# Causal convolution of the mLSTM queries and keys: read from its PSUM bank instead of from a padded copy in SBUF

## The reference, cut to what matters

```python
def causal_conv(x, w, b):
    K = w.shape[0]                                    # 4 taps
    S = x.shape[1]                                    # 256 tokens
    xp = jnp.pad(x, ((0, 0), (K - 1, 0), (0, 0)))
    return sum(xp[:, j:j + S] * w[j] for j in range(K)) + b
...
qk = jax.nn.silu(causal_conv(ml_qk, conv_w[l], conv_b[l]))   # ml_qk: 1024 channels
m_q, m_k = jnp.split(qk, 2, axis=-1)
```

## Time and profile before

| | |
|---|---|
| device time, median of 3 runs | 500.75 us (499.75 to 503.14) |
| the profiled execution | 500.96 us |
| its span, first to last instruction | 499.2 us |
| mean granted TensorE clock | 0.951 |
| busy: PE, DVE, ACT, POOL | 427.1, 165.3, 173.9, 157.9 us |
| DMA | 163.30 MB, mean 327 GB/s |

### The profile page before, as it was taken

One profiled execution on the slowest core, in us unless ns is written; L12 is line 12 of the kernel. 1 busy time (PEld: TensorE's weight loads), 2 busy tenths in 40 slices (PEclk: granted clock), 3 DMA queues, 4 the chain that ended last, 5 costly groups with the idle time before them and its releaser, 6 DMA issues.

```text
span 499.2 us, 8883 instructions
## 1 busy us (share of the span) xinstructions
PE 427.1 (86%) x3772; PEld 318.2 (64%) x3772; DVE 165.3 (33%) x345; ACT 173.9 (35%) x305; POOL 157.9 (32%) x126
## 2 busy tenths in 40 slices
PE   1837999899999999999996989898989788594983
PEld 0415989789899999997984745463636254261541
DVE  0224302899984232178236111111111111102014
ACT  1216451744549358534335331212122112030122
POOL 0008996574946865997700000000000000000000
PEclk9978999998999999999997999998989889799799
DMA  7999969579589347557999699999999999999942
GB/s 290 389 358 394 304 184 387 184 269 330 170 281 318 120 168 251 171 169 266 421 420 421 253 391 425 420 421 421 423 420 420 421 420 422 421 420 422 418 196 85
DMA packets 55725, 163.30 MB, mean 327 GB/s; under 512 B 7058, under 2 KB 33924, under 8 KB 43268
## 3 DMA queue, kind: packets, MB, share of 16 engines
q1 hardware_dynamic: 50528, 159.53, 82.7%
q10 hardware_dynamic: 5156, 3.17, 2.2%
HBM read 161.64 MB, written 1.05 MB: 326 GB/s over the span
## 4 chain that ended last, share of the span: by engine, by line
PE 70%; DMA 15%; DVE 5%; SPq 4%; issue 2%; ACT 2%; POOL 1%; DVEq 0%
PE bank L1271 33%; DMA ring<-in_w_e 11%; PE bank L1585 10%; PE bank L1597 7%; PE bank L1553 6%; PE bank L1542 5%; DMA ring<-in_w_ada 4%; PE bank L1224 3%; SPq L376 2%; SPq L365 1%; POOL ring_r L413 1%; DVE gm L1017 1%; PE bank L1508 1%; PE bank L1631 1%; PE bank L1560 1%
## 5 line engine op out<-in xcount | busy, mean ns | idle before, releaser
L413 POOL TENSOR_TENSOR ring_r<-ring,ring_r 128x512 fp32r<-128x512 f32 x120 | 157.6, 1348 | 89.1 <-ACT ring_r L448 88.9
L1271 PE MATMUL bank<-ring_r 128*128 128x256 f32 x832 | 111.3, 285 | 4.7 <-DVE att L837 2.3
L1271 PEld LDWEIGHTS bank<-ring_r 128*128 128x128 f32 x832 | 103.8, 191 | 7.4 <-issue 4.3
L670 ACT ACTIVATE raw<-bank,sm 128x128 f32<-128x128 f32 x72 | 27.2, 458 | 157.6 <-PE bank L1553 157.6
L448 ACT ACTIVATE ring_r<-ring 128x2048 fp32r<-128x2048 f32 x30 | 57.4, 1912 | 44.0 <-PE bank L1271 26.2
L1585 PE MATMUL bank<-ring,raw 128*32 128x256 f32 x640 | 57.0, 410 | 6.1 <-DMA hT<-in_w_e 6.1
L1149 DVE TENSOR_TENSOR tmp<-bank,tmp 128x256 f32<-128x256 f32 x8 | 3.4, 425 | 123.1 <-ACT tmp L678 123.1
L1585 PEld LDWEIGHTS bank<-ring,raw 128*32 128x32 f32 x640 | 28.2, 117 | 22.4 <-issue 10.7
L1553 PEld LDWEIGHTS bank<-const,xn 128*128 128x128 f32 x288 | 35.8, 199 | 9.0 <-issue 7.1
L1597 PE MATMUL bank<-ring,WT 128*32 128x512 f32 x160 | 37.5, 654 | 2.6 <-DVE WT L1154 2.6
L1224 PE MATMUL bank<-ring,sm 128*32 128x256 f32 x384 | 27.3, 433 | 13.9 <-DMA ring<-in_w_ada 13.7
(11 more groups left out here) (309 smaller groups left out, 591.7 us busy)
## 6 DMA issues: line engine op xcount, KB each, us to landing
ring<-in_w_e SPq DMA_DIRECT2D x60, 1024.0 KB, 24.7
ring<-in_w_ada SPq DMA_DIRECT2D x24, 1024.0 KB, 11.0
ring<-in_w_in SPq DMA_DIRECT2D x22, 1024.0 KB, 8.8
extra<-in_w_e SPq DMA_DIRECT2D x11, 1024.0 KB, 18.6
late<-in_w_e SPq DMA_DIRECT2D x5, 1024.0 KB, 19.3
qkT<-in_w_e SPq DMA_DIRECT2D x5, 1024.0 KB, 20.4
mqk<-in_w_e SPq DMA_DIRECT2D x5, 1024.0 KB, 26.2
gm<-in_w_e SPq DMA_DIRECT2D x5, 1024.0 KB, 26.1
```

The costliest lines, as they stand in the source:

```text
L413: pool.tensor_tensor(ring_r[:, slot_of(n), sl], ring[:, slot_of(n), sl], hi(d)[:, sl].bitcast(F32), ALU.subtract).then_inc(s["w_lo"], 1)
L670: ins = act.activation(xg[:, b, k, :], token_bank[:, j * P:(j + 1) * P], ACT.Identity, bias=S("B2p", KD)[:, k:k + 1], scale=S("A2p", KD)[: ...
L1271: ins = pe.matmul(out, left(k), right(k), start=(i == 0 and k == 0), stop=(i == 2 and k == nk - 1))
```

## The change

The padded copy is gone. The convolution reads the bank: the last tap (weight 3, no shift) is written to all 256 columns, and each other tap j, shifted back by 3 - j columns, is added to columns 3 - j and on, so that no zeros are needed. DVE's last instruction of `conv(i)` now releases the bank of `ml{i}`, ACT's four copies (L510) and POOL's clearing of the pads (L406) are dropped, and `conv(2)` and `conv(3)` are moved from behind the decay arguments to the place right behind `combine(3)`. ACT's Silu waits for the bank's release instead of for a semaphore of its own.

```diff
         def _(pool):
-            pool.memset(raw[:, :, 0:3], 0.0).then_inc(s["pads"], 1)
...
-                act.wait_ge(s["pads"], 1)
-                act.wait_ge(*full(f"ml{h}"))
-                release(act.activation(raw[:, 2 * h:2 * h + 2, 3:T + 3],
-                                       pb(f"ml{h}")[:].rearrange("p (a n) -> p a n", a=2), ACT.Copy), f"ml{h}")
                 split(9 + h)
...
-                act.wait_ge(s["conv_out"], i + 1)
+                act.wait_ge(*free(f"ml{i}"))
...
             def conv(i):
 
-                dve.wait_ge(*free(f"ml{i}"))
-                for k in (2 * i, 2 * i + 1):
-                    link(dve.tensor_scalar(mqk[:, k, :], raw[:, k, 3:T + 3], col("conv_w", 24 + k), col("conv_b", k),
-                                           ALU.mult, ALU.add))
+                job = f"ml{i}"
+                dve.wait_ge(*full(job))
+                for a in range(2):
+                    k, seq = 2 * i + a, pb(job)[:, a * T:(a + 1) * T]
+                    link(dve.tensor_scalar(mqk[:, k, :], seq, col("conv_w", 24 + k), col("conv_b", k), ALU.mult, ALU.add))
                     for j in range(3):
-                        ins = dve.scalar_tensor_tensor(out=mqk[:, k, :], in0=raw[:, k, j:j + T],
-                                                       scalar=col("conv_w", 8 * j + k), in1=mqk[:, k, :],
+                        back = 3 - j
+                        ins = dve.scalar_tensor_tensor(out=mqk[:, k, back:T], in0=seq[:, 0:T - back],
+                                                       scalar=col("conv_w", 8 * j + k), in1=mqk[:, k, back:T],
                                                        op0=ALU.mult, op1=ALU.add)
                         if j < 2:
                             link(ins)
-                    if k % 2 == 0:
+                    if a == 0:
                         link(ins)
-                ins.then_inc(s["conv_out"], 1)
+                release(ins, job)
...
             conv(1)
             combine(3)
+            conv(2)
+            conv(3)
...
             rows(2)
-            conv(2)
-            conv(3)
```

More of the change, by code:

```diff
@@ L506, in _ @@
                                    accum_out=S(f"Z{h % 2}", 4)[:, 2 * c + 1:2 * c + 2]).then_inc(s["pexp"], 1)
-                act.wait_ge(s["pads"], 1)
-                act.wait_ge(*full(f"ml{h}"))
-                release(act.activation(raw[:, 2 * h:2 * h + 2, 3:T + 3],
-                                       pb(f"ml{h}")[:].rearrange("p (a n) -> p a n", a=2), ACT.Copy), f"ml{h}")
                 split(9 + h)
-            act.wait_ge(s["pads"], 2)
+            act.wait_ge(s["pads"], 1)
             for i in range(2):
```

## The result

| | before | after |
|---|---|---|
| device time, median of 6 runs each | 500.25 us (498.77 to 503.14) | 508.51 us (505.97 to 513.99) |
| ratio after to before | | 1.0147, 95% interval [1.0121, 1.0173] |
| the profiled execution | 500.96 us | 509.3 us |
| its span | 499.2 us | 507.4 us |
| mean granted TensorE clock | 0.951 | 0.931 |

The kernel is slower by 1.5%, some 7.4 us. The forecast was 11.9 us slower, 512.9 us.

A forecast was written before the change was run, and what follows sets the result against it. PE was taken to bound the stretch. A later mv1 (10.46 us) plus its low clock (1.67) less the ada(2) wait (0.25) gave 11.9 us on 500.96, thus 512.9 us; range 508.5 to 516.5, more than 8 in 10.

The forecast's parts named there:

- PE is the bound, and every new wait is paid in full: From 89.9 to 224 us PE waits only 0.3 us, so any new wait of PE reaches the end.
- DVE as releaser of the banks: PE waits for convolution ends: some 5 us before mv0, 3 to 4 us before mv1.
- The third stall: PE's wait before the second transpose, aT1, for conv(2) to end at 133.2 us; 1 to 2 us.
- What a convolution costs: On DVE, an undisturbed convolution from PSUM takes 4.26 us (3.6 to 4.6) against 3.91, unstretched by POOL.
- the second rival: POOL stretches the PSUM reads of conv(2) and conv(3), 4.3 us more: 517.2 us; chance 0.06.
- DVE's line: DVE's queue of combine, columns and convolutions, followed with times from the trace before, ends conv(3) at 137.4 us.
- The term of 10.46 us: mv1 waits for conv(3) and starts at 137.45 instead of 126.99 us; this last stall holds the sum.
- the fourth rival: Faster: conv(1) would have to end before 118.94 us, but adaT4 makes 120.8 the earliest; chance 0.02.
- The clock: After PE's idle, mv1 begins at 1.2 GHz and takes 1.67 us more.
- the prediction's own signs of being wrong: mv0 near 119, convolutions at 1 us an operation, first expert load near 230 despite full waits, or clock 1.00 at mv1.
- the full one: Rival: the clock stays at 2.4 GHz in mv1, 511.2 us, or 509.2 with cheaper convolutions; chance 0.25.
- The saving of 0.25 us at `ada(2)`: PE's wait at ada(2) for own_columns to L904 on DVE goes away, 0.25 us less.

The follow-up runs named there:

- e4: Kernel after with another DVE order: conv(0) to conv(2) first, conv(3) behind columns(A2, 4), then combine(2), combine(3) and own_columns; 501.08 us, ratio 1.001.
- e1: Kernel before with only conv(2) and conv(3) moved right behind combine(3), still reading ACT's padded copies; 515.29 us, ratio 1.0311.
- before_again: Kernel before, unchanged, one more execution for a second trace; 506.43 us, beside 23 others with a median of 501.04 us.
- after_again: Kernel after, unchanged, measured and traced a second time; 508.21 us, ratio 1.0178.
- e2: Kernel before with conv(0) and conv(1) reading the bank; ml2 and ml3 still copied, conv(2) and conv(3) at their old place; 505.28 us, ratio 1.0097.
- e3: Kernel after with 24 extra matmuls of 256 columns before aT0, result thrown away; 508.7 us, and 510.66 us when run again.
- e7: Kernel before, copies kept, with the grow chain behind scores(1) and cols with the decay arguments ahead of conv(1); 502.4 us, ratio 1.002.
- e5: e4 with the chain of small operations on grow moved behind scores(1); 502.41 us, ratio 1.0036.
- e8: e7 with PE's small jobs spread: cols behind ml1, Mb0 behind ada(4), Mb1 behind ml2; 501.11 us, ratio 1.0012.
- e9: e8 with the router bias, which releases the bank of rb, ahead of conv(2); 498.78 us, ratio 0.9969.

## Why the prediction was right and where it was wrong

**PE is the bound, and every new wait is paid in full: right.** Of the waits at `mv0` and `mv1`, and of the slower `mv1`, nothing was absorbed: 7.02 later at `mv1`, 1.72 for its clock, and 0.3 for the wait at `ada(2)` that went, give 8.4; the first expert load is 8.34 late, the span 8.2. All other kernels keep the same 267 to 270 us from that load to the end of the span.

**The mechanism, DVE as releaser of the banks: right.** PE waits at `mv0` and `mv1` on the convolution's last operation, as said (3.5 and 2.7 us, where some 5 and 3 to 4 were forecast), and e4, in which only DVE's order differs, takes the loss back. The third stall, 1 to 2 us before the second transpose, did not come: `conv(2)` had ended at 129.7, ahead of `aT0`.

**What a convolution costs: right.** Forecast 4.26 us, measured 4.23 from the start of `conv(1)` to its end (118.41 to 122.64). `tensor_scalar` 544 ns, 535 assumed; `scalar_tensor_tensor` 481 ns, 485 assumed. No stretching under POOL, so the second rival (517.2 us) falls; e1 shows such stretching with the operands in SBUF, 515.29 us. The fixed extra cost for PSUM that the Trainium skill gives (VectorE: DVE Perf Modes, "The TRN2 errata — SBUF-src ops pay a fixed extra latency per instruction") and the prediction weighed is not seen for `scalar_tensor_tensor` (481 ns from PSUM, 485 from SBUF); `tensor_scalar` takes 130 ns more from PSUM (544 against 414).

**DVE's line: this is the step that failed.** The prediction read the durations of DVE's queue off one trace and kept them for the changed kernel. It took `conv(0)` at 110.8, `combine(2)` ending at about 119.6, `conv(1)` ending at 124.2 and "`combine(3)` takes the 4.71 us of today". Measured: 106.8, 112.9, 122.64 and 2.96. The term of 10.46 us was 7.02. Of the 3.4 us between them, 1.6 stood already at the end of `conv(1)`, 1.8 more were the shorter `combine(3)`, and the rest, under 0.2, are the convolutions and the start behind them. The first two come mostly from collisions with POOL that were read off the trace of before as if they were fixed times of these operations. They are not: POOL's units start when ACT's splits let them, and those start when PE fills a bank, so each shift of PE shifts them against DVE. The size of it shows without any change of code: 4.71 and 1.85 us for `combine(3)` with the order of before up to that place (the kernel before and e1; 6.5 in before_again), 2.96 and 1.85 after.

With the collisions of `combine(2)` gone, what bounds `mv0` is a loop that the fourth rival held: `adaT4` on PE (filled at 117.15), `columns(A2, 4)` and the operation behind it, `conv(1)`, and back to `mv0`. It stood in the text only to rule out a gain ("PE would wait 1.9 us"). It should have been the lower end of the forecast, with the contended line as the upper. As an estimate from the rows of before, the sum would then have been, at that end: `columns` 0.39 and `conv(1)` 4.26 us behind 116.8, thus 121.4, `combine(3)` between 2 and 4.7 us, two convolutions 8.5, `mv1` at 131.9 to 134.6, 4.9 to 7.6 us late. (Measured: 134.01 and 133.23.)

**The clock: half right, and in part luck.** The term was 1.67 us at `mv1`; it is 1.72 in the profiled execution and 0.2 in the second one, where the clock stayed at full, one of the prediction's own signs of being wrong. The text held both, the low clock at 0.62 and the full one at 0.25. The idle ahead was 2.69 us where the clock was low afterwards and 1.53 us where it stayed full. But the length of the idle does not decide alone, as `ml0` shows behind the same idle, first in e1, then in the kernel after:

```profile
88.59 2.15 PE L1271 MATMUL bank<-ring_r 128*128 128x256 f32 x16 [2.24 <-DVE att L837]
```
```profile
88.73 2.98 PE L1268 MATMUL bank<-ring_r 128*128 128x256 f32 x16 [2.32 <-DVE att L832]
```
Of the traces with this idle, the clock stays at 1.00 in all three in which ACT copies all four pairs (before, before_again, e1), and it falls to 0.50 in all six in which the first pair is read from its bank (after, after_again, e2, e4 and both of e3). So this is no chance of one trace, but what in the change brings it is not settled by these runs. Nor do small matmuls ahead of a job decide: in e7 the same eight (L1364) stand right before `mv0`, and it runs at full clock.

That slow `ml0` is a cost which the prediction did not have: the first 96 matmuls of `ml` take 13.08 us, the next 96 take 11.52. PE had begun them 1.15 us ahead of before (88.73 against 89.88) and reached `adaT4` 0.4 us behind it (116.76 against 116.39); e1, which began them at 88.59, reached it at 115.10. As `adaT4` stands in the loop to `mv0`, up to 1.6 us of the 7.02 can come from it; no run takes it alone. e4 has it too.

**The saving of 0.25 us at `ada(2)`: right**, and small.

**The range** (508.5 to 516.5 us) was set around a sum that was 3.5 us too high. The median of the six runs, 508.51, lies on its lower edge; by the ratio the time is 507.6 us (500.25 x 1.0147), and the second measurement gave 508.21, both below it. The waits came where they were forecast; their size did not.

## What to carry to other kernels

When a change hands the release of a buffer to a later engine, write down that engine's whole queue between two releases, not only the cost of the releasing operation: here the read from PSUM cost 0.3 us more for each undisturbed convolution and hurt nobody in e4, and the order of the queue cost some 7 us. Durations that contention stretches are no properties of the operations; forecast with both the undisturbed and the stretched one, and let the range hold both results. A trace or two more of the kernel before, taken ahead of the forecast, might have shown that spread. After a wait is removed, look for the next release on the same engine before counting the gain (e5 to e8 lost it all at the next bank, e9 kept half).

## What the runs showed of the hardware

An operation with one tensor in SBUF is not safe from POOL by that alone. `tensor_scalar` from SBUF to SBUF has a single input there, and in e1 its three instances beside POOL in the moved convolutions take 1.51, 1.27 and 1.35 us instead of 0.41. The trace of before had signs of it, with up to 0.88 us on L860. From PSUM it takes 531 to 544 ns beside POOL and without. Undisturbed, `tensor_scalar` from SBUF takes 0.29 us for 128 columns and 0.35 for 256 (L845 and its like in `combine`), half a nanosecond for a column, where `scalar_tensor_tensor` takes one (0.35 and 0.48). The Trainium skill ("SBUF — State Buffer", section "Who interferes with whom") says that `tensor_scalar` can enter a mode that uses the port pair shared with GpSimd, and that the one that comes first holds the pair for its whole instruction. The traces agree: the form that takes half a nanosecond for a column is the one that collides, and a stretched instance lasts about as long as one piece of POOL (16.49 us for 12 in e1, 1.37 each). The prediction named "two tensors in SBUF" as the condition, and was right on PSUM for a reason that covers only part of the cases.

Operations on very few columns are hit too: L880 in the kernel after, 8 columns with both tensors in SBUF, takes 0.99 us beside POOL, where its like (L883 of the kernel before, at 120.31) takes 0.17 us.

Also not expected was how far DVE's line differs between two executions of the same code. The order of before gave `combine(3)` 4.71 us in one execution and 1.85 us in another (e1), and `combine(2)` 3.6 and 5.7 us, each by where it met POOL's units.
